# Three engines' written order of steps changed from the first norm to the end, and the PSUM banks of the levels swapped in the last HGRN2 group

## The reference, cut to what matters

```
x  -> conv_gdn_mixer: proj = x @ w_in; gated short conv (A) and gated DeltaNet (B, 8 heads, chunks of 64)
   -> layer_norm(sqrt(2) * x + y @ w_out), then x += (p @ w_pl) * sigmoid(x @ w_pl_gate)
   -> hgrn2_mixer: 16 heads, f = lb + (1 - lb) * sigmoid(f_raw), S_t = diag(f_t) S_{t-1} + k_t v_t^T, o_t = S_t^T q_t
   -> layer_norm(...), the same gate again
   -> second block: mod = silu(c) @ w_ada; rms norm; 6 fox heads, 4 mLSTM heads, 6 MoBA heads; @ w_out
   -> rms norm; (silu(h @ gate) * (h @ up)) @ w_down, added to x
```

## Time and profile before

| | us |
|---|---|
| median of 3 runs (lowest, highest) | 1065.51 (1065.23, 1066.73) |
| the profiled execution | 1066.17 |
| its span, first to last instruction | 1064.4 |
| TensorE busy (matmul) | 1026.2, 96% |
| weight loads | 902.2, 85% |
| VectorE | 752.0, 71% |
| ScalarE | 542.4, 51% |
| mean granted TensorE clock | 0.991 |

### The profile page before, as it was taken

How to read it: one execution, slowest core, us unless ns; L and a number is a source line. 1 busy time by engine, 2 the same in 40 slices (tenths; PEclk the granted TensorE clock), 3 DMA queues, 4 the chain that set the end, 5 groups by cost and what they waited for, 6 DMA issues and landing times.

```text
span 1064.4 us, 21569 instructions
## 1 busy us (share of the span) xinstructions
PE 1026.2 (96%) x9120; PEld 902.2 (85%) x9120; DVE 752.0 (71%) x1049; ACT 542.4 (51%) x601; POOL 0.5 (0%) x7
## 2 busy tenths in 40 slices
...
GB/s 348 159 183 157 159 120 119 120 127 178 93 80 284 236 232 121 158 87 196 143 143 120 156 192 158 319 332 195 122 186 129 119 237 159 198 198 168 169 171 46
DMA packets 26302, 181.47 MB, mean 170 GB/s; under 512 B 3040, under 2 KB 3296, under 8 KB 4960
## 3 DMA queue, kind: packets, MB, share of 16 engines
...
...
## 4 chain that ended last, share of the span: by engine, by line
PE 80%; DVE 10%; ACT 6%; issue 2%; DMA 1%; ACTq 0%; SPq 0%; DVEq 0%
PE PS L910 77%; ACT WH L1380 2%; DVE WL L1791 2%; PE PS L1073 1%; PE PS L1151 1%; DMA layer<-xt 1%; DVE X L1987 1%; DVE X L1988 1%; DVE layer_ln L2101 1%; ACT L1726 1%; PE PS L1301 1%; DVE STAT L1969 0%; DVE X L1968 0%; DVE layer L2094 0%; DVE layer L2095 0%
## 5 line engine op out<-in xcount | busy, mean ns | idle before, releaser
L910 PE MATMUL PS<-XTH,WH 128*128 128x256 f32 x1392 | 404.9, 291 | 4.1 <-ACT WH L1380 1.8
L910 PE MATMUL PS<-XTL,WH 128*128 128x256 f32 x1392 | 395.3, 284 | 0.0
L910 PE MATMUL PS<-XTH,WL 128*128 128x256 f32 x1392 | 395.2, 284 | 0.0
L1791 DVE TENSOR_TENSOR WL<-RAW,WH 128x2048 fp32r<-128x2048 f32 x138 | 314.2, 2277 | 109.5 <-ACT WH L1380 106.3
L1380 ACT ACTIVATE WH<-RAW 128x2048 fp32r<-128x2048 f32 x138 | 262.6, 1903 | 194.1 <-PE PS L910 190.2
L910 PEld LDWEIGHTS PS<-XTH,WH 128*128 128x128 f32 x1392 | 268.4, 193 | 9.1 <-issue 4.3
L910 PEld LDWEIGHTS PS<-XTL,WH 128*128 128x128 f32 x1392 | 268.6, 193 | 2.3 <-issue 2.2
L910 PEld LDWEIGHTS PS<-XTH,WL 128*128 128x128 f32 x1392 | 268.4, 193 | 0.0
L910 PE MATMUL PS<-WH,YH 128*128 128x512 f32 x224 | 89.6, 400 | 1.1 <-DVE YL L2266 1.1
L910 PE MATMUL PS<-WH,YL 128*128 128x512 f32 x224 | 87.4, 390 | 0.0
L910 PE MATMUL PS<-WL,YH 128*128 128x512 f32 x224 | 87.3, 390 | 0.0
...
## 6 DMA issues: line engine op xcount, KB each, us to landing
RAW<-wst SPq DMA_DIRECT2D x162, 1024.0 KB, 4.9
...
```

The costliest lines, as they stand in the source:

```text
L910: return pe.matmul(o, lhsT, rhs, start=start, stop=stop)
L1791: tt(WL[:, i % RAW_RING, 0:n], RAW[:, i % RAW_RING, 0:n], as_float(WH[:, k % SPLIT_RING, 0:n]), ALU.subtract).then_inc(vector_done, 1)
```

## The change

**Banks.** In the last group of HGRN2 the even levels take banks 0 and 1, and the odd ones 2 and 3; in the other groups it stays the other way round.

```diff
         for i in range(NL):
-            out.append((later(step, "hm", g, i, on="T", banks=(0, 1) if i % 2 else (2, 3), readers="V",
+            out.append((later(step, "hm", g, i, on="T", banks=(0, 1) if (i + (g == HGRN_GROUPS - 1)) % 2 else (2, 3), readers="V",
                               read_in=("hp", g, i)), 1.0))
```

```diff
 ORDER_T
- v:1:0 gk:0 first:v:1:1 v:1:1 first:q:1:0 gkk:0
+ first:v:1:1 v:1:0 v:1:1 gk:0 gkk:0 first:q:1:0
- first:zb:1:1 first:ah:1:1 zb:1:1 vtr:1
+ first:ah:1:1 first:zb:1:1 zb:1:1 vtr:1
- gx:1:2:0 gp:1:3:0 gx:1:1:1 out:0:1:1 gu:1:2:1 gu:1:3:0 gx:1:2:1 gp:1:3:1 gx:1:3:0 gp:1:4:0 gu:1:3:1
+ gx:1:1:1 gx:1:2:0 gp:1:3:0 gu:1:2:1 gu:1:3:0 gp:1:3:1 gx:1:2:1 gx:1:3:0 gp:1:4:0 gu:1:3:1 out:0:1:1
- first:f:1:1 hm:0:3 f:1:1
+ first:f:1:1 f:1:1 hm:0:3
- hr:2:0 hd:3 i:3:0 first:i:3:1 i:3:1 hm:3:0
+ hd:3 hr:2:0 i:3:0 hm:3:0 first:i:3:1 i:3:1
- hm:3:4 ada:3:1 hm:3:5 adat:3
+ hm:3:4 ada:3:1 adat:3 hm:3:5
- grow:4 first:feat:5 feat:5 feat:6
+ first:feat:5 feat:5 grow:4 feat:6
- ada:10:0 ada:10:1 xt:5:0 xt:5:3 xt:5:2 ada:11:0 xt:5:1
+ ada:10:0 xt:5:2 ada:10:1 ada:11:0 xt:5:0 xt:5:3 xt:5:1
- ff:0 ff:1 ff:2 ff:3 ff:5 ff:4 ff:6 ff:7 ff:8 ff:9
+ ff:1 ff:0 ff:2 ff:3 ff:5 ff:4 ff:6 ff:8 ff:7 ff:9
 ORDER_S
- split:102:124 val:1:1 turn:6 pv:5 turn:7
+ turn:6 pv:5 turn:7 val:1:1
- rms:1:0:0 rms:1:0:1 rms:1:1:0 rms:1:1:1
+ rms:1:0:0 rms:1:1:0 rms:1:0:1 rms:1:1:1
- split:113:139 split:112:138 ff:5 ff:4
...
+ split:113:139 ff:4 ff:5 split:112:138
 ORDER_V
- hy:0:2 hp:0:0 split:51:58 hp:0:1 split:53:60 hy:0:3
+ hp:0:0 split:51:58 hy:0:2 hp:0:1 split:53:60 hy:0:3
- hy:2:3 hp:2:1
+ hp:2:1 hy:2:3
- hr:2:0 hd:3 hy:3:1 split:75:82 hy:3:2 hp:3:1 hp:3:0 hp:3:2 hy:3:3 split:76:85 hy:3:4
+ hd:3 hy:3:1 hr:2:0 hp:3:0 hy:3:2 split:75:82 hy:3:3 hp:3:1 split:76:85 hy:3:4 hp:3:2
- first:out2:1:1 rmsb:1:0 out2:0:1 out2:1:1 rmsb:1:1
+ out2:0:1 first:out2:1:1 out2:1:1 rmsb:1:0 rmsb:1:1
- ff:4 ff:3 split:112:138 split:113:139 ff:5 ff:6
+ ff:4 ff:3 split:113:139 split:112:138 ff:6 ff:5
```

More of the change, by code:

```diff
@@ L473 @@
 ba first:k:0:0 k:0:0 first:k:0:1 k:0:1 first:v:0:0 v:0:0 norm:k:0 first:v:0:1 v:0:1 gcc first:q:0:0 q:0:0 first:q:0:1
[L474 to L492, removed]
@@ new lines @@
+gp:0:3:0 gx:0:2:1 ac:0:1 gu:0:3:0 first:az:0:1 gu:0:3:1 gp:0:4:0 gx:0:3:0 gx:0:3:1 gp:0:4:1 gu:0:4:0 az:0:1 gu:0:4:1
+gp:0:5:0 gx:0:4:0 first:ab:0:1 gu:0:5:0 gp:0:5:1 gx:0:4:1 gx:0:5:0 gp:0:6:0 gu:0:5:1 ab:0:1 first:ah:1:0 gu:0:6:0
+gp:0:6:1 gx:0:5:1 gv:0:0 ah:1:0 gs:0 first:ac:1:0 gu:0:6:1 gks:0 ac:1:0 gv:0:1 first:az:1:0 go:0 az:1:0 gr:0:0
+first:zb:1:0 first:ab:1:0 ab:1:0 zb:1:0 gc:1 first:ah:1:1 first:zb:1:1 zb:1:1 vtr:1 norm:q:1 first:ac:1:1 ah:1:1
+first:az:1:1 ac:1:1 gk:1 az:1:1 gkk:1 first:ab:1:1 ab:1:1 gp:1:0:1 gp:1:0:0 out:0:0:0 gu:1:0:1 gu:1:0:0 out:0:1:0
@@ L519 @@
[L519 to L523, removed]
@@ new lines @@
+split:25:25 gs:0 split:26:26 gv:0:1 gq:0:0 split:27:27 gr:0:0 split:28:28 az:1:0 zb:1:0 split:29:29 gc:1 zb:1:1
+split:30:30 norm:q:1 split:31:31 split:32:32 ah:1:1 split:33:33 az:1:1 split:35:35 split:34:34 split:36:36 gx:1:1:0 xl
+gx:1:1:1 gx:1:2:0 gx:1:2:1 gx:1:3:0 gx:1:3:1 gx:1:4:0 gx:1:4:1 gx:1:5:0 split:38:38 gv:1:0 gx:1:5:1 gs:1 split:37:37
+lb gv:1:1 split:39:39 gq:1:0 gq:1:1 gr:1:0 gr:1:1 pl:0:0 lna:0:0 xt:0:0:0 lna:0:1 pl:0:1 split:40:45 xt:0:0:1 ada:0:1
+xt:0:1:0 split:41:46 ada:1:1 xt:0:1:1 split:42:47 first:gate:0:0:1 split:43:48 gate:0:0:1 first:gate:0:1:1 split:44:51
@@ L581 @@
-split:119:145 ff:11 ff:10 split:120:146 split:121:147 ff:12 split:122:148 ff:13 ff:14 split:123:149 ff:15 ff:16
-split:124:150 split:125:151 ff:17 split:126:152 ff:18 split:127:153 ff:19 ff:20 split:128:154 split:129:155
-split:130:156 split:131:157 ff:21 split:132:158 split:133:159 split:134:160 split:135:161 first:down:0:5 down:0:5
-split:136:162 split:138:164 split:137:163 first:down:1:5 down:1:5
+split:6:6 q:0:0 v:0:1 gcc split:7:7 q:0:1 split:8:8 gc:0 split:9:9 split:10:10 k:1:0 split:11:11 vtr:0 norm:q:0
@@ new lines @@
+gc:1 split:29:29 split:30:30 vtr:1 gc2:1 norm:q:1 gk:1 split:31:31 ac:1:1 gkk:1 split:32:32 ab:1:1 gp:1:0:0 gp:1:0:1
+split:33:33 gu:1:0:1 gu:1:0:0 split:34:34 gp:1:1:0 gp:1:1:1 gu:1:1:0 gp:1:2:0 split:35:35 gu:1:1:1 split:36:36
+gu:1:2:0 gp:1:2:1 gp:1:3:0 gu:1:2:1 gu:1:3:0 gp:1:3:1 gu:1:3:1 gp:1:4:0 gu:1:4:0 wg gp:1:4:1 gp:1:5:0 gu:1:4:1
+gu:1:5:0 gp:1:5:1 gp:1:6:0 setup gu:1:5:1 gu:1:6:0 gp:1:6:1 split:38:38 gks:1 gu:1:6:1 lb lb2 split:37:37 gz:1 c1
+split:39:39 gr:1:0 gr:1:1 first:out:0:0:3 first:out:0:1:3 lna:0:0 lnb:0:0:0 out:0:0:3 out:0:1:3 lna:0:1 xt:0:0:0
```

144 lines of the change are left out of this document (78 added, 66 removed).

## The result

The changed kernel takes 1057.3 us (median of 4 runs, 1055.1 to 1057.78) beside 1065.74 in the same session: ratio 0.9911, 95% interval 0.9899 to 0.9923. Forecast were 1058.0 and 1054.5 to 1063.5. The medians differ by 8.4 us. Forecast were 7.5. In later sessions the kernel before had medians of 1066.0 to 1066.8.

The account below looks back on a forecast made before the run. TensorE, busy 1026.2 of 1064.4 us, was taken as the bound, with gains only from its idle time and half-clock stretches. Terms summed to −7.5: 1066.17 became 1058.7, less 0.66 gave 1058.0; range 1054.5 to 1063.5.

Parts of the forecast that it names:

- overlap: All TensorE waits: each one removed is worth up to 0.15 us more than its bracket; taken as −0.8 in total.
- gkk:0 and first:ah:1:1: DeltaNet: new waits of +1.1 at gkk:0 and +0.95 at first:ah:1:1, with −0.37 returned at vtr:1.
- The inverse's levels: DeltaNet: four waits of 0.22 go, one of 0.25 comes, first:ah:0:1 saves 0.1; net −0.7 us.
- The first HGRN2 group: At hm:0:3: the wait of 1.81 goes (−1.8 us), and the half-clock stretch behind it goes too (−1.6).
- Third group: Third HGRN2 group: waits of 0.25 at hm:2:3 and 0.32 at hm:2:5 go, −0.6 us.
- Last group: Last HGRN2 group: four waits totalling 5.31 us go, 2.3 left at hm:3:3, hm:3:4 and adat:3; net −3.0.
- Norm: Last norm: the wait of 2.62 us becomes about 2.8 and ends earlier by as much as is owed; 0.
- rival D: Feed-forward: splits come later than their units want them, kernel slower, 1069.0 us at 0.5 a unit; chance 0.06.
- B: HGRN2 levels: VectorE sets the pace, so the HGRN2 groups' gains halve; 1061.5 us, chance 0.15.
- C: Later in the kernel: TensorE runs into loads or splits paced by HBM, undoing the gain; about 1065 us, chance 0.09.
- A: Near 420 us: the half-clock stretch stays although the wait at hm:0:3 goes; 1059.6 us, chance 0.17.
- main line: Whole kernel: the summed terms hold, including the clock stretch going with hm:0:3's wait; 1058.0 us, chance 0.53.

Follow-up runs that it names:

- DeltaNet alone: Kernel before with all new orders up to the end of xt:1 (DeltaNet and its norm), the rest as before: 1065.38 us, ratio 0.9993.
- banks alone: Kernel before with only the bank swap of the last HGRN2 group, all orders as before: 1066.35 us, ratio 0.9996.
- TensorE's or VectorE's swap alone: Kernel before with f:1:1 ahead of hm:0:3 on TensorE (1064.1 us), or hp:0:0 and split:51 ahead of hy:0:2 on VectorE (1063.78 us).
- last group: Kernel before with the last HGRN2 group's bank swap and new orders of all three engines, hr:2:0 to mod:0: 1062.63 us, ratio 0.9958.
- orders only: Kernel before with the last HGRN2 group's new orders, without the bank swap and the two moves that need it: 1061.36 us, ratio 0.9954.
- first group back: Changed kernel with the first HGRN2 group's orders as before: 1059.78 us, ratio to the kernel before 0.9937.
- the five built on it: Changed kernel with two DeltaNet places restored, ada:10:1 restored, both plus ada:11:0 moved, norm rewritten, or gp:0:0:0 also later: 1054.94, 1055.13, 1054.52, 1053.86, 1053.06 us.

## Why the prediction was right, and where it was not

**The bound** was read rightly: TensorE's idle time and its half-clock windows. The profile after has 5.1 less idle time and 3.3 less busy time with the same matmuls. Of the busy time only 1.5 was forecast; the rest was not taken apart. A part of it is the prediction's overlap: an unhindered matmul starts up to 0.15 us before its predecessor's modelled end, while ahead of a wait all of that end counts as busy.

**The sum** came out at −7.5 beside −8.4, and luck has a part in that: the first block was 1.9 better than its term, the third group 1.2 worse, and the −0.8 for overlap has no row of its own in the table, since it lies in the others.

**gkk:0 and first:ah:1:1**: forecast +1.1 and +0.95 with −0.37; measured +1.3 and +1.0 with −0.55. Both were right, and in the profile of the run that takes them back both brackets are gone. What its expectation missed is that the wait at gkk:0 took the place of one of 0.57 at gp:0:0:0.

**The inverse's levels** were mis-sized: forecast −0.7, measured −1.3 in each group of four heads. One part is the price of a bracket. From the start of gu:0:4:1 to the start of gp:0:5:0 it is 0.86 us before and 0.51 after, so the bracket of 0.22 cost 0.35:

```profile
162.42 0.64 PE L910 MATMUL PS<-layer,layer_x 128*64 128x64 f32 x16
163.28 0.69 PE L910 MATMUL PS<-layer_x,layer 128*64 128x64 f32 x16 [0.22 <-DVE layer_x L1923]
```

```profile
163.19 0.69 PE L910 MATMUL PS<-layer,layer_x 128*64 128x64 f32 x16
163.70 0.64 PE L910 MATMUL PS<-layer_x,layer 128*64 128x64 f32 x16
```

The other part is brackets below 0.2, which the timeline does not print and the prediction did not count: up to gx:1:5:0, the second group had six of 0.17 to 0.22 in all and has four. These do not add up to the whole 2.6; the rest lies in many changes of less than 0.2 between steps that now follow one another otherwise, and was not assigned. So the first block was 0.9 faster, where the sum had it 1.0 slower.

**The first HGRN2 group**: forecast −1.8 and −1.6, measured −3.5. The size was right and its mechanism half right. The wait accounts for 2.0 (the run with the old orders there), the clock for 1.5, as the prediction had it by count. Each swap alone removes the wait, by experiment, but for 0.29 or 0.85. That the clock fell just here in the profiled execution is another matter, see below.

**Third group**: forecast −0.6; the two brackets did go, and behind hm:2:3 the profile wins 0.6, but hm:2:3 itself takes 1.57 and not 0.54 from its first matmul to its last, with a pause that no releaser explains. Its term came out at +0.6 with what else lies between f:1:1 and i:3:0.

**Last group**: forecast −3.0 from 5.31 less 2.3 left over; left over are 2.03, place by place as forecast. The step that failed is "by the swap hm:3:0 ... can start a value unit ahead, and hd:3 and hy:3:1 go before hr:2:0": as cause of the gain it is worth 0.5. The other 2.7 come with the orders behind it, VectorE's above all: hp:3:0 ahead of hy:3:2, so that hm:3:2's bank is free, with split:75 behind hy:3:2, and adat:3 ahead of hm:3:5 on TensorE. The runs with the swap alone (0.9996) and the orders alone (0.9954) show it. The rows were also misread in two places. hr:2:0's 1.70 of waiting lies ahead of 583.65 and not within the 5.6. And an hp takes 1.32 in the first two levels and 0.70 only from the third on, an hy there 1.7 to 2.0 and not 1.6:

```profile
597.03 2.65 DVE L2101 COPY_PREDICATED layer_ln<-CST,PS 128x512 f32<-128x512 uint32 x2
600.71 0.70 DVE L2101 COPY_PREDICATED layer_ln<-CST,PS 128x512 f32<-128x512 uint32 x1 [1.03 <-PE PS L910]
```

So VectorE's 4.6 a level was too short for the first levels, and that the waits left over came out place by place is in part luck.

**Heads, attention**: −0.3 and −0.4, measured −0.6 and −0.7. No run took these two apart. **Norm**: 0, measured +0.2, but not by the wait that was forecast: it is 3.80 and not 2.8, nor "under 3". The 0.65 that stood ahead of ada:10:0 and the 0.9 of ada:10:1 went into it, and XN comes 0.4 earlier. **Feed-forward, down**: no bracket behind 866, rival D has fallen. But of the 0.7 to 1.1 us between split and unit, left by hand, ff:8 has 0.26 (split:113 ends at 904.45, the unit starts at 904.71) and ff:18 0.37; the others have 0.78 and more. **Table loads, moved DMAs**: nothing of them shows in TensorE's waits; no run tested them alone. **Range**: its lower end is 1054.8 by its own terms (1058.0 − 2.3 − 0.9), not 1054.5; nothing hangs on it.

**The rivals.** B (VectorE sets the pace) would have left over 3 us of waits in the last group; 2.03 are left. C did not come: behind the first 18 us no wait over 0.1 of TensorE in the profile after is ended by a DMA. A, the clock, is the interesting one. Counted over the fourteen profiled executions of this case, in the HGRN2 groups (410 to 620 us):

| waits of 1.7 to 2.2 us left in the kernel | executions | waits together | windows of 0.50 there |
|---|---|---|---|
| three (before, DeltaNet alone, banks alone) | 3 | 9 | 1 + 2 + 3 |
| two (TensorE's or VectorE's swap alone) | 2 | 4 | 1 + 1 |
| one (last group, orders only, first group back) | 3 | 3 | 0 |
| none (the changed kernel and the five built on it that keep its first group) | 6 | 0 | 0 |

In the one with orders only, the window that holds the wait at hm:0:3 has TensorE busy 1.59 of 3.40 just as in the kernel before, and the next one is at 1.00:

```profile
417.40:420.80 3.40, 1.59 (x72) 1.39 (x71) 3.30 (x5) 2.25 (x3) 0.00 (x0) 1.00 0.99 407
420.80:424.20 3.40, 3.40 (x31) 3.40 (x30) 3.30 (x5) 0.00 (x0) 0.00 (x0) 1.00 0.06 22
```

So a window of 0.50 follows half of such waits (8 of 16), and no stretch of levels without one; which wait it follows changes from one execution to the next. The waits of 1.24 to 1.28 at first:f:2:1, one in each of the fourteen executions, have no such window behind them. Outside these groups the share differs from wait to wait. Ahead of xt:0:1:1 near 342 us eight of the executions have a wait of 1.69 or 1.70, and none a window behind it; ahead of xt:4:0 near 700 all have one of 1.96 to 2.25, and six of fourteen a window; at the last norm, with waits of 2.1 to 3.8, thirteen of fourteen. The main line's −1.6 was right as an amount, since the change removes all three waits (half of three, at 1.5 each, is an estimate of 2.2), but not as tied to hm:0:3. Much of the runs' spread goes with it: twenty executions of the kernel before went from 1063.99 at a mean clock of 0.994 to 1068.56 at 0.988; those at 0.993 and 0.994 took up to 1065.54, those at 0.991 and 0.992 from 1066.09 to 1067.9. The last 1.8 us between executions at the same clock are something else. What decides it between equal waits stays open; moving a wait in time by a chosen amount, which would test it, was not tried.

The rule cited for rival A from the Trainium skill ("TensorE: Matmul & The Clock Gate", "HAM oscillation — how this bites in real kernels") does not agree with these executions: the clock fell behind waits of 1.7 to 2.1 us, shorter than the gaps it names.
